# Hybrid attention and MLP block: last ten attention steps reordered, squares added on VectorE, first weights in three groups, unit-matrix products on TensorE before x

## The chip, the cores and the metric

The kernel runs on one core of a Trainium2 chip. The metric is the device time of one execution in microseconds (us), the median of several executions.

## What is computed

One encoder layer for a sequence of 1024 tokens and a model width of 1024, all in float32. The residual stream is normalised, projected to queries, keys and values of two head groups, both groups attend within chunks of 64 tokens, the heads go through one output projection, and a squared-ReLU MLP follows.

```
h = rmsnorm(x, g_pre_mix)
proj = h @ w_in + b_in            # 1024 x 2304: aq, ak, av, bq, bk, bv
out_a = sliding-window attention of 8 heads over 2 chunks, shared keys, a sink per head, bucket bias
out_b = attention of 8 heads over own + 8 previous chunks, bias by clipped relative distance
y = concat(out_a, out_b) @ w_out
x = x + rmsnorm(y, g_post_mix)
h = rmsnorm(x, g_pre_mlp)
y = square(relu(h @ w_up)) @ w_down      # width 4096
out = x + rmsnorm(y, g_post_mlp)
```

## The kernel before

Every engine has its own program, written out by hand as one list of instructions; there is no scheduler. The programs meet at counting semaphores: `wait_ge(s, n)` holds an engine until the semaphore s has reached n. So the order in the code is the order on each engine, and a wait holds all that stands behind it on that engine. A float32 product is made as three products of split operands (`three`, L1621 to L1626): high by high, high by low, low by high. The high part is a rounded copy that ScalarE (ACT) writes, the low part is the difference, which VectorE (DVE) writes.

**First stage.** The sum over the model width goes in eight pieces k of 128 columns. For each k, SyncE (SP) loads 512 KB of x (`load_x`), TensorE (PE) turns its eight 128x128 blocks by products with the unit matrix `ident` into banks 6 and 7 of PSUM (`x_transposes`, T(k) below), ACT writes `x_hi`, DVE writes `x_lo`, and PE makes 18 products of the piece with the first three weight tiles (`first_products`). T(k+1) overwrites the banks that x_hi and x_lo of k are read from, so it waits for x_lo(k). The weights of a piece are 192 KB (`w1_raw`), loaded in two groups by `load_first_weights`: k = 0 and 1 from ACT's queue, k = 2 to 7 from SP's; each is five transfers. ACT also squares x piece by piece (`square`) into two alternating buffers `sq`, which GpSimd (POOL) adds to `sumsq` (L761). A square from k = 3 on waits for the addition two before it. Ahead of the additions POOL's program builds two bias tables, `arow` and `brow`, from small transfers (`relrow`, `t5row`). The sum is reduced (L1140), rooted on ACT and inverted on DVE; its diagonal form `diag` is multiplied on PE (L1662) behind the products of k = 6, after a wait for x_lo of k = 7.

**Attention.** It runs over 64 steps n of one pair of heads and 128 queries: 32 of group A, then 32 of group B, where the keys of a step grow from 128 to 640 over the eight steps of a pair. In each step PE makes the scores of n, `weigh(n-2)` (probabilities by values), and the transposes of the probabilities of n-1, in up to three chunks; between the chunks it makes part of 256 "fills": products of values 2 to 7 and of ten more projection tiles. The fills end with step 53. DVE adds the bias and finds the row's maximum (`scores`), and divides by the row sums (`normalize`); ACT makes the exponentials (`exp`). The transposed chunks are copied out of PSUM by ACT (chunks 0 and 1) and DVE (the last one). Up to step 53 all chunks use bank 6; from step `LATE` = 54 on they rotate over three banks. Scores of group B have one buffer in PSUM: PE's scores(n) wait for DVE's scores(n-1). DVE also takes finished fills out of PSUM (`values`, 320 columns, 12 times; `tile_scaled`, 512 columns, 20 times in the steps), and in the last steps ACT and DVE split the eight pieces of `w_out` (`wo_high`, `wo_low`), at the steps that WO_STEPS lists. Every fourth step ACT stores four finished outputs (`store_mix`).

**After it** come the output projection (`out_steps`, `out_tile`), the norms, and the two MLP products by a scheme of seven products of half-size matrices. The change doesn't touch them.

## Time and profile before

| what | us |
|---|---|
| median of 3 runs | 1135.88 (1135.09 to 1138.67) |
| the profiled execution | 1134.49 |
| its span | 1132.6 |
| TensorE busy | 1078.2 (95%) |
| VectorE busy | 788.1 (70%) |
| ScalarE busy | 473.2 (42%) |
| GpSimd busy | 224.6 (20%) |

The span is what the engines' instructions cover, and 1.9 us lie around it. TensorE does something 95% of the time, so only stretches in which it stands still or in which its granted clock is low have time to give.

### The profile page before, as it was taken

The numbers are of one execution on the slowest core, as the hardware profiler recorded it, in microseconds if no ns is written. First come the engines' busy times: TensorE is split into PE (matmuls) and PEld (weight loads), VectorE is DVE, ScalarE is ACT, GpSimd is POOL, SyncE is SP. The second block draws the span as 40 slices with busy tenths as digits, with TensorE's granted clock in tenths as the row PEclk, the third lists the DMA queues.
The fourth block names the chain that finished last, engine by engine and source line by source line (L and its number), as shares of the span: only waits on it lengthen the run. The fifth ranks groups of instructions, "written<-read, shape, count | busy, mean of one in ns | idle before, by whom it ended". The sixth has DMA issues, their size and how long they took to land.

```text
span 1132.6 us, 16339 instructions
## 1 busy us (share of the span) xinstructions
PE 1078.2 (95%) x5772; PEld 881.2 (78%) x5772; DVE 788.1 (70%) x1634; ACT 473.2 (42%) x951; POOL 224.6 (20%) x195
## 2 busy tenths in 40 slices
PE   6999999999997699998999999999999999999995
PEld 5798877777875588876788888888888888778884
DVE  2754466676766646579898888887544586677797
ACT  4522355544445545584231313131244444344552
POOL 5400000000000000031866667575300000000000
PEclk9999999999998899998999999999999999999998
DMA  9350111111106012221444453535777753354343
GB/s 258 86 173 1 29 30 61 43 38 43 43 1 205 1 60 102 82 92 65 166 141 162 145 168 139 174 133 196 242 251 241 234 148 93 117 181 153 98 117 152
DMA packets 80544, 137.79 MB, mean 122 GB/s; under 512 B 16568, under 2 KB 32960, under 8 KB 78416
## 3 DMA queue, kind: packets, MB, share of 16 engines
q1 hardware_dynamic: 79104, 136.35, 37.3%
q8 instruction: 47, 0.77, 0.3%
q10 hardware_dynamic: 1360, 0.39, 0.2%
q14 instruction: 33, 0.27, 0.1%
HBM read 98.93 MB, written 42.51 MB: 125 GB/s over the span
## 4 chain that ended last, share of the span: by engine, by line
PE 83%; DVE 6%; issue 4%; ACT 3%; POOL 2%; SPq 1%; DMA 1%; ACTq 0%; DVEq 0%; POOLq 0%
PE ps L1624 24%; PE ps L1626 23%; PE ps L1625 23%; PE ps L1747 4%; PE ps L1731 4%; PE ps L1713 3%; ACT prob_b L888 1%; DVE b_lo L1338 1%; PE ps L1825 1%; POOL arow L749 1%; DVE probT_b L1251 1%; SPq L319 1%; DVE wc_lo L1349 1%; DVE tm_lo L1536 1%; DVE sm_lo L1534 0%
## 5 line engine op out<-in xcount | busy, mean ns | idle before, releaser
L1624 PE MATMUL ps<-b_hi,wc_hi 128*128 128x512 f32 x448 | 176.0, 393 | 7.5 <-DVE wc_lo L1349 5.2
L1624 PE MATMUL ps<-tm_hi,sm_hi 128*128 128x512 f32 x448 | 175.1, 391 | 2.8 <-DVE tm_lo L1536 2.5
L1626 PE MATMUL ps<-b_hi,wc_lo 128*128 128x512 f32 x448 | 175.8, 392 | 0.0
L1625 PE MATMUL ps<-b_lo,wc_hi 128*128 128x512 f32 x448 | 175.6, 392 | 0.0
L1626 PE MATMUL ps<-tm_hi,sm_lo 128*128 128x512 f32 x448 | 174.4, 389 | 0.0
L1625 PE MATMUL ps<-tm_lo,sm_hi 128*128 128x512 f32 x448 | 174.4, 389 | 0.0
L1090 ACT ACTIVATE sm_hi<-sm_raw 128x512 fp32r<-128x512 f32 x112 | 70.7, 631 | 152.5 <-DMA sm_raw<-u_matrices 152.5
L1534 DVE TENSOR_TENSOR sm_lo<-sm_raw,sm_hi 128x512 fp32r<-128x512 f32 x112 | 77.1, 689 | 76.4 <-ACT sm_hi L1090 75.9
L1624 PEld LDWEIGHTS ps<-b_hi,wc_hi 128*128 128x128 f32 x448 | 84.9, 190 | 26.8 <-DVE wc_lo L1349 3.8
L1624 PEld LDWEIGHTS ps<-tm_hi,sm_hi 128*128 128x128 f32 x448 | 84.1, 188 | 23.6 <-issue 3.3
L1625 PEld LDWEIGHTS ps<-b_lo,wc_hi 128*128 128x128 f32 x448 | 84.8, 189 | 17.8
L1626 PEld LDWEIGHTS ps<-b_hi,wc_lo 128*128 128x128 f32 x448 | 84.8, 189 | 17.6
L1626 PEld LDWEIGHTS ps<-tm_hi,sm_lo 128*128 128x128 f32 x448 | 84.1, 188 | 17.6
L1625 PEld LDWEIGHTS ps<-tm_lo,sm_hi 128*128 128x128 f32 x448 | 84.1, 188 | 17.2
L1349 DVE TENSOR_TENSOR wc_lo<-wc_raw,wc_hi 128x512 fp32r<-128x512 f32 x64 | 72.1, 1129 | 7.6 <-POOL wc_raw L791 5.5
L1536 DVE TENSOR_TENSOR tm_lo<-w,tm_hi 128x512 fp32r<-128x512 f32 x112 | 76.5, 683 | 0.0
L782 POOL TENSOR_TENSOR wc_raw<-up_raw 128x512 f32<-128x512 f32 x16 | 25.3, 1584 | 251.7 <-PE ps L1794 176.2
L1048 ACT ACTIVATE p1s<-ps 128x512 f32<-128x512 f32 x16 | 9.5, 596 | 154.8 <-PE ps L1626 151.9
L1099 ACT ACTIVATE tm_hi<-w 128x512 fp32r<-128x512 f32 x112 | 69.1, 617 | 0.0
L1624 PE MATMUL ps<-x_hi,wf_hi 128*128 128x512 f32 x160 | 67.6, 422 | 0.1
L1626 PE MATMUL ps<-x_hi,wf_lo 128*128 128x512 f32 x160 | 63.0, 394 | 0.0
L876 ACT ACTIVATE probT_b<-ps 128x512 f32<-128x512 f32 (+3 forms) x48 | 25.9, 540 | 87.6 <-PE ps L1731 87.6
(195 smaller groups left out, 2201.3 us busy)
## 6 DMA issues: line engine op xcount, KB each, us to landing
u_matrices<-stage SPq DMA_DIRECT2D x112, 256.0 KB, 2.4
sm_raw<-u_matrices SPq DMA_DIRECT2D x112, 256.0 KB, 2.6
up_raw<-in_w_up SPq DMA_DIRECT2D x16, 1024.0 KB, 5.9
w<-in_w_down SPq DMA_DIRECT2D x64, 256.0 KB, 3.8
xraw<-in_x SPq DMA_DIRECT2D x8, 512.0 KB, 6.3
w_raw<-in_w_in SPq DMA_DIRECT2D x8, 512.0 KB, 3.5
xr<-in_x SPq DMA_DIRECT2D x8, 512.0 KB, 3.5
x_rows<-xr SPq DMA_DIRECT2D x8, 512.0 KB, 2.6
```

Source lines behind the costliest of these rows:

```text
L876: nc.scalar.activation(dst, src, ACT.Copy).then_inc(s_pta, 1)
L1090: nc.scalar.activation(sm_hi[r][:], sm_raw[r][:], ACT.Copy).then_inc(s_shi, 1)
L1099: nc.scalar.activation(tm_hi[r][:], down_weights[q][c][:], ACT.Copy).then_inc(s_thi, 1)
L1349: nc.vector.tensor_tensor(wc_lo[s][p][:], src, wc_hi[s][p][:].bitcast(F32), ALU.subtract).then_inc(s_wlo[s], 1)
L1534: nc.vector.tensor_tensor(sm_lo[r][:], sm_raw[r][:], sm_hi[r][:].bitcast(F32), ALU.subtract).then_inc(s_slo, 1)
L1536: nc.vector.tensor_tensor(tm_lo[r][:], down_weights[q][c][:], tm_hi[r][:].bitcast(F32), ALU.subtract).then_inc(s_tlo, 1)
L1624: pe.matmul(out, w_hi_, x_hi_, start=start, stop=False)
L1625: pe.matmul(out, w_hi_, x_lo_, start=False, stop=False)
L1626: return pe.matmul(out, w_lo_, x_hi_, start=False, stop=stop)
L1713: last = pe.matmul(score_of(n, hh)[:, c * width:(c + 1) * width], q[rows, tok], k[rows, keys], start=(i == 0), stop=(i == 2))
L1731: last = pe.transpose(ps[:, bank, i * P:(i + 1) * P], prob_of(n, hh)[:, c0 + k * P:c0 + (k + 1) * P], ident[:])
L1747: last = pe.matmul(ps[64 * hh:64 * hh + 64, 7, (t % 4) * P:(t % 4) * P + P], v_tok[:, t + 1 - nk + k, at + 64 * hh:at + 64 * hh + 64], pro ...
```

## The change

It has six parts. (1) PE multiplies the unit matrix by itself 14 times before T(0) and 24 times between T(0) and T(1), into a bank that the first real product overwrites. (2) The first weights are loaded in three groups, k = 0, k = 1 and 2, and k = 3 to 7, and SP's loads stand in another order. (3) ACT and DVE split the weights of k = 0 before they touch x(0). (4) The seven additions of squares move from POOL to DVE. (5) In all attention steps DVE empties finished fills before it works on the scores. (6) From step 54 on PE transposes before it weighs, ACT makes both exponentials before it copies a chunk, and DVE copies its chunk before it normalises; WO_STEPS puts five pieces of w_out, not three, behind the last step.

The tables and the loads of SP:

```diff
-WO_STEPS = (55, 57, 59, 61, 63, 64, 64, 64)
+SQUARES = ((0,), (1,), (2, 3), (4,), (5, 6), (7,), (), ())
+
+WO_STEPS = (59, 61, 63, 64, 64, 64, 64, 64)
...
-            k0, k1 = ((0, 2), (2, KT))[g]
+            k0, k1 = ((0, 1), (1, 3), (3, KT))[g]
...
             load_first_weights(sp, 1)
+            load_x(2)
+            load_x(3)
+            load_first_weights(sp, 2)
+            for k in range(4, KT):
+                load_x(k)
             sp.dma_start(relrow[:, 0:513], rel).then_inc(s_tab, 16)
             sp.dma_start(t5row[:], t5).then_inc(s_tab, 16)
-            for k in range(2, KT):
-                load_x(k)
```

ACT, first stage (`first_hi`, which is new, stands once ahead of the wait for x and then behind it), and attention:

```diff
+            def first_hi(k):
+                act.wait_ge(s_w1[(k >= 1) + (k >= 3)], 80)
+                nc.scalar.activation(w1_hi[:, k], w1_raw[:, k], ACT.Copy).then_inc(s_w1hi, 1)
...
             for k in range(KT):
+                if k == 0:
+                    first_hi(0)
                 act.wait_ge(s_xt, k + 1)
                 nc.scalar.activation(x_hi[:, k], two(6), ACT.Copy, scale=g1[:, k:k + 1]).then_inc(s_xhi, 1)
-                act.wait_ge(s_w1[k >= 2], 80)
-                nc.scalar.activation(w1_hi[:, k], w1_raw[:, k], ACT.Copy).then_inc(s_w1hi, 1)
...
+                if k:
+                    first_hi(k)
...
-                if 1 <= n <= STEPS:
+                if 1 <= n < LATE:
                     copy_chunk(n - 1, 0)
...
-                    for c in range(1, len(chunks_of(n - 1))):
+                    for c in range(0 if n >= LATE else 1, len(chunks_of(n - 1))):
```

DVE, first stage (the same addition leaves POOL's program; `first_lo` goes as `first_hi`), and attention:

```diff
+            def add_squares(k):
+                dve.wait_ge(s_sq, k + 1)
+                if k >= 2:
+                    dve.wait_ge(s_acc, k - 1)
+                total = sumsq[:].rearrange("p t n -> p (t n)")
+                nc.vector.tensor_tensor(total, total, sq[:, k % 2], ALU.add).then_inc(s_acc, 1)
...
+                if k >= 2:
+                    for n in SQUARES[k - 1]:
+                        add_squares(n)
...
-                if n < STEPS:
-                    scores(n)
...
                 if n < STEPS:
+                    scores(n)
+                if n >= LATE:
+                    copies_of(n - 1)
+                if n < STEPS:
                     for hh in range(2):
                         normalize(n, hh)
```

PE, first stage and attention:

```diff
+            def keep_awake(times):
+
+                for _ in range(times):
+                    pe.transpose(ps[:, 0, 0:P], ident[:], ident[:])
+
             pe.wait_ge(s_id, 2)
+            keep_awake(14)
             x_transposes(0)
+            keep_awake(24)
...
-                if n >= 2:
+                if 2 <= n < LATE:
                     weigh(n - 2)
...
+                if n >= LATE:
+                    weigh(n - 2)
```

Three places show how the order moves. The first is DVE's program for k = 2 to 5 of the first stage; before:

```order
L1133 SCALAR_TENSOR_TENSOR x_lo<-ps,small,x_hi 128x1024
L1136 TENSOR_TENSOR w_lo<-w_raw,w_hi 128x384
L1133 SCALAR_TENSOR_TENSOR x_lo<-ps,small,x_hi 128x1024
L1136 TENSOR_TENSOR w_lo<-w_raw,w_hi 128x384
L1127 TENSOR_TENSOR wv_lo_108<-wv_raw_100,wv_hi_92 128x640
```

and with the change, k = 2 to 4 (wv_lo are the low parts of the value weights):

```order
L1150 SCALAR_TENSOR_TENSOR x_lo<-ps,small,x_hi 128x1024
L1135 TENSOR_TENSOR w_lo<-w_raw,w_hi 128x384
L1143 TENSOR_TENSOR sumsq<-sumsq,sq 128x1024
L1150 SCALAR_TENSOR_TENSOR x_lo<-ps,small,x_hi 128x1024
L1135 TENSOR_TENSOR w_lo<-w_raw,w_hi 128x384
L1143 TENSOR_TENSOR sumsq<-sumsq,sq 128x1024 x2
L1150 SCALAR_TENSOR_TENSOR x_lo<-ps,small,x_hi 128x1024
L1135 TENSOR_TENSOR w_lo<-w_raw,w_hi 128x384
L1143 TENSOR_TENSOR sumsq<-sumsq,sq 128x1024
L1130 TENSOR_TENSOR wv_lo_108<-wv_raw_100,wv_hi_92 128x640
```

One or two additions of 1024 columns now stand behind each w_lo, and one of them stands ahead of the reduction of the sum. The second place is PE's program of steps 62 and 63; before, the second half of the scores (bk, bq), weigh (probT_b by v_tok) and then the transposes (ident, prob_b):

```order
L1713 MATMUL ps<-bk_hi_57,bq_hi_53 128x320 x2
L1713 MATMUL ps<-bk_lo_59,bq_hi_53 128x320 x2
L1713 MATMUL ps<-bk_hi_57,bq_lo_55 128x320 x2
L1747 MATMUL ps<-probT_b,v_tok 64x128 x10
L1731 MATMUL ps<-ident,prob_b 128x128 x10
L1713 MATMUL ps<-bk_hi_57,bq_hi_53 128x320 x2
```

and with the change:

```order
L1745 MATMUL ps<-bk_hi_57,bq_hi_53 128x320 x2
L1745 MATMUL ps<-bk_lo_59,bq_hi_53 128x320 x2
L1745 MATMUL ps<-bk_hi_57,bq_lo_55 128x320 x2
L1763 MATMUL ps<-ident,prob_b 128x128 x10
L1779 MATMUL ps<-probT_b,v_tok 64x128 x10
L1745 MATMUL ps<-bk_hi_57,bq_hi_53 128x320 x2
```

The transposes of step n-1 no longer stand behind weigh(n-2) and its waits. The third place is ACT's program of steps 61 to 63; before:

```order
L876 ACTIVATE probT_b<-ps 128x512
L888 ACTIVATE prob_b,small<-prob_b,small 128x640 x2
L876 ACTIVATE probT_b<-ps 128x512
L900 ACTIVATE wo_hi<-wo_raw 128x1024
L895 ACTIVATE mix<-ps 128x4x128
L876 ACTIVATE probT_b<-ps 128x512
L888 ACTIVATE prob_b,small<-prob_b,small 128x640 x2
L876 ACTIVATE probT_b<-ps 128x512 x2
L888 ACTIVATE prob_b,small<-prob_b,small 128x640 x2
```

and with the change:

```order
L891 ACTIVATE prob_b,small<-prob_b,small 128x640 x2
L879 ACTIVATE probT_b<-ps 128x512 x2
L903 ACTIVATE wo_hi<-wo_raw 128x1024
L898 ACTIVATE mix<-ps 128x4x128
L891 ACTIVATE prob_b,small<-prob_b,small 128x640 x2
L879 ACTIVATE probT_b<-ps 128x512 x2
L891 ACTIVATE prob_b,small<-prob_b,small 128x640 x2
```

The two exponentials of a step (L888, then L891) stood between the copies of the chunks 0 and 1 (L876), and now stand ahead of both.

## Rows read from the trace of the kernel before

**Rows 1.** Windows: busy us and count of each engine, granted clock, DMA share, GB/s

```profile
0.00:11.50 11.50, 3.44 (x15) 3.10 (x16) 1.90 (x3) 4.07 (x5) 0.86 (x7) 1.00 0.97 217
...
51.60:341.20 289.60, 285.00 (x2063) 230.05 (x2061) 178.71 (x660) 129.75 (x332) 4.19 (x20) 1.00 0.15 49
341.20:398.90 57.70, 39.62 (x367) 31.65 (x367) 38.10 (x119) 30.17 (x67) 0.00 (x0) 0.86 0.33 101
398.90:500.00 101.10, 101.10 (x488) 84.04 (x487) 60.56 (x141) 59.72 (x118) 7.24 (x5) 1.00 0.26 93
...
363.00:375.00 12.00, 9.51 (x58) 7.08 (x59) 9.13 (x30) 4.87 (x13) 0.00 (x0) 0.61 0.01 1
```

**Rows 2.** Waits of TensorE, 341.2 to 398.9 us: total, times, longest

```profile
PE ps L1747 <- DVE probT_b L1251: 10.7, 8, 2.9
PE ps L1747 <- ACT mix L895: 4.6, 2, 2.6
PE ps L1731 <- ACT probT_b L876: 2.1, 2, 1.4
```

**Rows 3.** Waits of TensorE, 51.6 to 341.2 us

```profile
PE ps L1624 <- DVE v_tok L1185: 1.7, 4, 0.6
```

**Rows 4.** Timeline of the first stage: start, length, engine, instruction, idle time before it

```profile
5.29 1.94 PE L1633 MATMUL ps<-ident,xraw 128*128 128x128 f32 x8 [5.29 <-DMA xraw<-in_x]
...
9.77 0.52 ACT L841 ACTIVATE w_hi<-w_raw 128x384 fp32r<-128x384 f32 x1 [1.33 <-DMA w_raw<-in_w_in]
...
10.00 1.94 PE L1633 MATMUL ps<-ident,xraw 128*128 128x128 f32 x8 [2.77 <-DVE x_lo L1133]
...
14.32 0.55 DVE L1136 TENSOR_TENSOR w_lo<-w_raw,w_hi 128x384 fp32r<-128x384 f32 x1
...
20.34 2.56 DVE L1136 TENSOR_TENSOR w_lo<-w_raw,w_hi 128x384 fp32r<-128x384 f32 x1
...
25.36 1.06 ACT L828 ACTIVATE sq<-xraw 128x1024 f32<-128x1024 f32 x1 [4.90 <-POOL sumsq L761]
...
41.63 1.03 PE L1633 MATMUL ps<-ident,xraw 128*128 128x128 f32 x8
...
45.52 1.21 DVE L1140 TENSOR_REDUCE small<-sumsq 128x8 f32<-128x1024 f32 x1
...
46.60 1.04 PE L1633 MATMUL ps<-ident,xraw 128*128 128x128 f32 x8
...
49.80 1.27 DVE L1133 SCALAR_TENSOR_TENSOR x_lo<-ps,small,x_hi 128x1024 fp32r<-128x1024 f32 x1
...
51.61 1.88 PE L1662 MATMUL ps<-diag,ones 128*128 128x512 f32 x4
```

**Rows 5.** Groups by line of GpSimd, 0 to 60 us

```profile
L761 POOL TENSOR_TENSOR sumsq<-sumsq,sq 128x1024 f32<-128x1024 f32 x7 | 17.6, 2509 | 2.4 <-ACT sq L828 1.7
...
L752 POOL TENSOR_SCALAR brow<-relrow 8x384 f32<-8x384 f32 x1 | 1.2, 1163 | 0.0
```

**Rows 6.** Timeline of the late steps, one engine at a time

```profile
342.52 0.82 DVE L1228 CUSTOM_DVE_ANT_0 prob_b<-ps,bias_b 128x640 f32<-128x640 f32 x1
...
378.36 0.82 DVE L1228 CUSTOM_DVE_ANT_0 prob_b<-ps,bias_b 128x640 f32<-128x640 f32 x1
...
380.79 0.82 ACT L888 ACTIVATE prob_b<-prob_b,small 128x640 f32<-128x640 f32 x1
...
383.22 0.42 DVE L1251 COPY probT_b<-ps 128x256 f32<-128x256 f32 x1
383.98 1.23 DVE L1255 TENSOR_TENSOR wo_lo<-wo_raw,wo_hi 128x1024 fp32r<-128x1024 f32 x1 [0.34 <-ACT wo_hi L900]
...
384.58 1.31 PE L1747 MATMUL ps<-probT_b,v_tok 128*64 128x128 f32 x20 [2.59 <-ACT mix L895]
385.82 1.31 PE L1731 MATMUL ps<-ident,prob_b 128*128 128x128 f32 x10
...
398.94 0.78 PE L1624 MATMUL ps<-wo_hi,mixr_hi 128*128 128x512 f32 x1
```

More of the change, by code:

```diff
@@ L406, in build @@
         s_xlo = sem("x_lo_ready")
-        s_w1 = [sem(f"first_weights_landed{n}") for n in range(2)]
+        s_w1 = [sem(f"first_weights_landed{n}") for n in range(3)]
         s_w1hi = sem("first_weights_hi_ready")
@@ L755, in _ @@
                                     ).then_inc(s_rows, 1)
-            for k in range(1, KT):
-                pool.wait_ge(s_sq, k + 1)
-                if k >= 2:
-                    pool.wait_ge(s_acc, k - 1)
-                nc.gpsimd.tensor_tensor(sumsq[:].rearrange("p t n -> p (t n)"), sumsq[:].rearrange("p t n -> p (t n)"),
-                                        sq[:, k % 2], ALU.add).then_inc(s_acc, 1)
             for p in range(8):
@@ L833, in value_hi @@
                 nc.scalar.activation(wv_hi[k][:], wv_raw[k][:], ACT.Copy).then_inc(s_wvhi, 1)
-            squares = ((0,), (1,), (2, 3), (4,), (5, 6), (7,), (), ())
+            def first_hi(k):
+                act.wait_ge(s_w1[(k >= 1) + (k >= 3)], 80)
+                nc.scalar.activation(w1_hi[:, k], w1_raw[:, k], ACT.Copy).then_inc(s_w1hi, 1)
             act.wait_ge(s_g1, 16)
             for k in range(KT):
+                if k == 0:
+                    first_hi(0)
                 act.wait_ge(s_xt, k + 1)
                 nc.scalar.activation(x_hi[:, k], two(6), ACT.Copy, scale=g1[:, k:k + 1]).then_inc(s_xhi, 1)
-                act.wait_ge(s_w1[k >= 2], 80)
-                nc.scalar.activation(w1_hi[:, k], w1_raw[:, k], ACT.Copy).then_inc(s_w1hi, 1)
-                for n in squares[k]:
+                if k:
+                    first_hi(k)
+                for n in SQUARES[k]:
                     square(n)
@@ L1128, in value_lo, with first_lo @@
                                         ).then_inc(s_wvlo, 1)
+            def first_lo(k):
+                dve.wait_ge(s_w1hi, k + 1)
+                nc.vector.tensor_tensor(w1_lo[:, k], w1_raw[:, k], w1_hi[:, k].bitcast(F32), ALU.subtract
+                                        ).then_inc(s_w1lo, 1)
+            def add_squares(k):
[4 more added lines that the diff above has]
+                nc.vector.tensor_tensor(total, total, sq[:, k % 2], ALU.add).then_inc(s_acc, 1)
             dve.wait_ge(s_g1, 16)
             for k in range(KT):
+                if k == 0:
+                    first_lo(0)
                 dve.wait_ge(s_xhi, k + 1)
@@ L1134, in _ @@
                                                in1=x_hi[:, k].bitcast(F32), op0=ALU.mult, op1=ALU.subtract).then_inc(s_xlo, 1)
-                dve.wait_ge(s_w1hi, k + 1)
-                nc.vector.tensor_tensor(w1_lo[:, k], w1_raw[:, k], w1_hi[:, k].bitcast(F32), ALU.subtract
-                                        ).then_inc(s_w1lo, 1)
+                if k:
+                    first_lo(k)
+                if k >= 2:
+                    for n in SQUARES[k - 1]:
+                        add_squares(n)
                 if k == KT - 2:
@@ L1251, in copy_chunk, with copies_of @@
                 nc.vector.tensor_copy(dst, src).then_inc(s_ptd, 1)
+            def copies_of(n):
+                for c in range(len(chunks_of(n))):
+                    if not chunks_of(n)[c][2]:
+                        copy_chunk(n, c)
             def wo_low(k):
@@ L1277, in _ @@
                         tile_lo(m - V_HALVES + 2 * FIRST_TILES)
-                for c in range(len(chunks_of(n - 1)) if n else 0):
-                    if not chunks_of(n - 1)[c][2]:
-                        copy_chunk(n - 1, c)
+                if 1 <= n < LATE:
+                    copies_of(n - 1)
                 for j in range(FILL_TILES):
```

## The prediction

> **What bounds the kernel now.** First I read the windows [rows 1], which give busy time and granted clock of TensorE (PE) by stage. From 51.6 to 341.2 us it is busy 285.0 of 289.6 us, and behind 398.9 us it is full: 101.1 of 101.1. What these stretches hold can only move as a block. The late attention steps, 341.2 to 398.9 us, are different: 39.62 busy of 57.70, so 18.1 us stand still, at a mean granted clock of 0.86; between 363 and 375 us it is 0.61. Then I read the waits of that stretch [rows 2]: 15.3 of its us are `weigh` waiting, 10.7 for the copy of a chunk by VectorE (DVE) and 4.6 for `store_mix` on ScalarE (ACT). The reader is to see that the engine named is not slow; PE's program has put weigh(n-2) ahead of the transposes of n-1, and DVE's copy stands behind its normalisation. In the middle PE waits 1.7 us for fills to leave PSUM [rows 3]. Last comes the timeline of the first stage [rows 4]: PE starts T(0) when x(0) lands (5.29), T(1) at 10.00 behind x_lo(0), and from there every piece costs 46.60 - 41.63 = 4.97 us if nothing stops PE. Something does: ACT stood 4.90 us before the square at 25.36, held by POOL's additions, with x_hi of the next piece queued behind it.
>
> **First stage.** The end of the stage is the product with `diag` at 51.61 [rows 4].
>
> Loads. ACT's five transfers for k = 0 and 1 landed at 9.77. At a mean 217 GB/s over the first 11.5 us [rows 1] that is about 2.1 MB, in which two pieces of x (1.0 MB), 0.4 MB of ACT's group and 0.6 MB of SP's are seen to be under way. With groups of one and two pieces some 1.4 MB stand ahead of k = 0's last byte, so I estimate its landing at 7.0 us (6 to 8.5: it shares the queues with x(1)). This matters, because ACT now waits for it ahead of x_hi(0). T(0) ends at 5.29 + 1.94 = 7.23 in any case, so the new wait costs about 0.3 us (nothing to 1.7): w_hi 0.5, x_hi 1.1, x_lo 1.3 give x_lo(0) at about 10.1, where T(1) starts today.
>
> Unit-matrix products. T(0) has 8 in 1.94 us, or 0.24 each; 14 of them are 3.4 us and hide before 5.29. The 24 behind T(0) cost 5.8 us at that pace and would hold T(1) until 13.0; at the pace of T(7), 8 in 1.04, they cost 3.1 and end at 10.3. The truth lies between, since the ends overlap: I take T(1) at 10.1 and keep 11.7 for the range. Behind it the clock is up: T(1) costs 1.0, not 1.94, and the 18 long products of k = 0 take 4.1 us, as any piece's do (4.97 less some 0.85 for the next T). T(2) then starts near 15.0, and at 4.97 a piece T(7) at 39.8 instead of 46.60: 6.8 us to win if PE is never held.
>
> Additions. On POOL one takes 2.51 us [rows 5]. On DVE the nearest row is wo_lo, same size and both inputs in SBUF: 1.23 us [rows 6]. DVE's list for a piece is x_lo 1.3, w_lo 0.5, one or two additions, and from k = 4 a wv_lo of 0.8: 5.0 us at most in a period of 4.97. It just fits. But ACT's second square of a piece waits for an addition (squares 3, 6, 7), and x_hi of the next piece stands behind it on ACT. Walking the lists: x_hi is 0.4 us late at k = 3, 1.0 at k = 5, 1.7 at k = 6. PE has about 1.5 us of slack, so T(7) slips by 0.1 only. What is late next is the tail: the reduction stood 45.52 - 41.63 = 3.9 us behind T(6) and now has the later x_lo(6) and an addition ahead of it (2.9 us more), and x_lo(7), which PE needs before `diag`, is behind the reduction, root and diag in DVE's list. It ended at 51.07 with PE at 51.61, so 0.5 us of slack; of 6.8 us won 4.5 stay. PE waits some 2.3 us there.
>
> The port. w_lo of 384 columns took 2.56 us at 20.34, while POOL ran `brow`, and 0.55 at 14.32 [rows 4]. By the Trainium skill, "SBUF — State Buffer", section "Who interferes with whom", a DVE instruction with two SBUF inputs contends with a GpSimd instruction that reads SBUF, and the one that starts second blocks; the additions are of that kind. By it the additions that meet the tables would stretch; without it they cost 1.23. The rows bound it: two `brow` instructions of 1.16 us [rows 5] delay DVE by at most 2.3 us once, now near 31 us where PE's slack takes most. I take 0.5 us. First stage: 4.5 - 0.5 = **4.0 us won**, between 1.5 and 6.8.
>
> **Middle steps.** DVE's program before fill n was: wait for PE's scores, then empty the fill. Now it empties first, while it waits. The fills are done on PE before the scores, so this fits the wait. At most the 1.7 us of [rows 3] come back. At worst each of 12 value halves (about 0.45) and 20 tile halves (0.69) delays a chain: 19 us; but PE was busy 98.4% of this stretch, and the probabilities of a step were ready some 2.6 us before PE reached their transposes. I take **0.8 us won**.
>
> **Late steps.** The cycle today, by [rows 6]: DVE's scores(61) start at 378.36, and the first exponential could start 0.9 us later, but ACT has the copy of chunk 0 of step 60 ahead of it, for which PE's transposes must run: 380.79, 1.6 us late. Then PE holds at weigh(60) until 384.58, and the transposes of 61, whose probabilities were ready at 383.2, start at 385.82.
>
> New cycle of a full step, from DVE's scores start s: second half done s + 1.6; exponentials 0.85 to 2.6; DVE copies its chunk until 1.95, normalises until 2.7 and 3.45. PE: scores of the next step from 1.65 to 2.85 (weigh and transposes take 1.24 each, from 384.58 to 385.82 and on), transposes from 3.1 (ACT's copies free the bank) to 4.4, weigh to 5.7, and again scores. Period 5.7 - 1.65 = about 4.1 us, set by PE. In a step with wo_low (59, 61, 63) ACT's wo_hi ends at s + 4.6 and DVE goes on at 5.8: period 5.8. Steps 56 to 59 have few keys and take 2.6 to 4.8.
>
> Step 54 pays first. The chunks of step 53 still share bank 6, and their copies are now behind ACT's exponentials: transposes at 342.3, 345.7 and 346.9, and DVE normalises only at 347.7 (345.6 today). Its PE idles 2.8 us. From there, with scores(54) at 342.5, the DVE scores of 55 to 63 start at 350.0, 353.3, 356.6, 359.1, 361.7, 366.5, 369.9, 375.7 and 379.0. The last transposes follow at 382.4, weigh(62) at 383.8, and the output projection when wo_low(2) and the low half of mix are made, 386.1, instead of 398.94: 12.8 us. Five pieces of w_out behind the last step cost nothing: DVE makes one in 1.2 us, PE uses one in six products of 512, about 1.4 us, and has weigh(63) to do as well.
>
> Against it stands the clock. Gaps of 2 to 2.6 us in today's late steps were followed by a granted clock of 0.61 over twelve us [rows 1]. The walk has gaps of 2.8 us (step 54) and 1.9 us (step 60), and at 1.2 GHz the 3.7 us of PE work in a step become 7.4. The Trainium skill, "TensorE: Matmul & The Clock Gate", Part 1, says that the clock is throttled by default and activity releases it; so a stage with fewer gaps should keep it, and here the rows agree that it falls behind gaps. I take 2 us off (0 to 5). Late steps: **10.8 us won**, between 6 and 15; 18.1, all idle time, is the ceiling.
>
> **Sum**, on the profiled execution's own time: 1134.49 - 4.0 - 0.8 - 10.8 = 1118.9, so 1119. The median of the runs lies 1.4 us above that execution, which is inside the runs' own spread. Behind 398.9 nothing changes and PE is full, so the block moves up whole.
>
> **Rivals.** (a) As walked, both ends gain: 1119, 1113 to 1125. Chance 0.60. (b) Everything overlaps better, clock up throughout and no wait for `diag`: 1134.5 - 6.8 - 1.7 - 15 = 1111. For it: PE's work in the late steps is under 39.6 us. Against: DVE's list with wo_low. 0.14. (c) The late clock stays at half, or the copies hold the transposes in most steps: late gain 5, so 1134.5 - 4 - 0.8 - 5 = 1125. 0.12. (d) DVE's additions and POOL's tables get in each other's way: each addition that meets the 9 us of tables stretches as w_lo did, by 2.0 us; some four do, three of them feed ACT's squares, and the first stage gains nothing: 1134.5 - 11.6 = 1123. For it: w_lo at 20.34. Against: the short `arow` instructions, running since 13.8, did not stretch w_lo at 14.32. 0.07. This is the case in which the rule of the SBUF page decides. (e) It does nothing: a transfer or table with a fixed time catches the shifted block, 1134. Against: SP's later loads wait for semaphores of the engines that move with it. 0.04. (f) Slower: step 54's pattern repeats in all ten late steps, because both exponentials stand ahead of the copies that free a bank. Price 2.1 us a step, with today's waits kept: 1134.5 - 4.8 + 21 = 1151. It decides when a bank comes free later than the probabilities are ready; with three banks I get 0.3 us, not 2. 0.03.
>
> **Numbers.** What a measurement of this kernel can tell from no change is about 0.3%, 3.4 us. Faster by more than that are (a) to (d) and nothing of (e): 0.93; within, 0.04; slower, 0.03. The range reaches from (b) to (c) and a little past: 1111 to 1127.
>
> **What would show it.** T(1) near 10 us and T(7) near 40, both with products at 0.23 us pitch; PE idle about 2 us before the product with `diag`; DVE additions at 1.2 us; no ACT wait on additions over 2 us. In the late steps: weigh no longer waits, exponentials start 0.9 us behind DVE's scores, the stage from PE's scores(54) to the first output product lasts 45 us, not 57.7, and step 54 is the longest wait. I am wrong if T(1) starts after 12 us, if the late stage is longer than 52 us, or if the span from the first output product to the end changes by over 1 us.

## The result: 20 us faster, 1.7%

| | before | after |
|---|---|---|
| median | 1136.39 (4 runs, 1135.09 to 1138.67) | 1116.23 (4 runs, 1115.60 to 1119.44) |
| ratio | | 0.9826, 95% interval 0.9801 to 0.9851 |
| the profiled execution | 1134.49 | 1116.27 |
| its span | 1132.6 | 1114.4 |

The forecast was 1119.0 in a range of 1111 to 1127. Timed a second time (e10 below) the changed kernel took 1120.05 us, 14.9 less than the kernel before beside it, so the change is worth 15 to 20 us. The two profiled executions differ by 18.2 us. First the engines' busy time in the changed kernel, with its share of the span:

```profile
PE 1075.4 (97%) x5810; PEld 879.5 (79%) x5810; DVE 795.6 (71%) x1641; ACT 475.1 (43%) x951; POOL 209.8 (19%) x188
```

TensorE's busy time is nearly that of before, unit products and all; its share rises because the span shrank around it. To see where, I read four places in each trace: the first value product (the first after the first stage), PE's scores of step 54, the first output product, and the end.

| us | before | after | gain |
|---|---|---|---|
| first value product | 57.45 | 54.94 | 2.5 |
| from there to PE's scores(54) at 341.19 and 336.21 | 283.74 | 281.27 | 2.4 |
| from there to the first output product (the late stage) | 57.75 | 45.71 | 12.0 |
| from there to the end of the span (the rest) | 733.66 | 732.48 | 1.2 |

Windows of the changed kernel (busy us and count of PE, PEld, DVE, ACT and POOL, granted clock, DMA share, GB/s), which answer to [rows 1]. The first has the length of the middle window there, but starts inside the first stage; the second is the late stage exactly:

```profile
46.00:336.00 290.00, 284.83 (x2064) 230.56 (x2063) 183.07 (x671) 131.61 (x335) 4.21 (x20) 1.00 0.16 51
...
336.21:381.92 45.71, 36.88 (x367) 28.63 (x367) 35.01 (x118) 29.29 (x66) 0.00 (x0) 0.93 0.42 128
```

The late stage runs the same 367 products as in [rows 1]. PE now stands still for 8.8 of its us, not 18.1, and its work takes 36.9 us instead of 39.6 because the granted clock is 0.93 instead of 0.86. So 9.3 us of the 12.0 are waits that went, and 2.7 us are the same products at a higher clock.

**Late steps.** PE's waits of the changed kernel, 336 to 392 us:

```profile
PE ps L1763 <- ACT probT_b L879: 4.8, 5, 2.7
PE ps L1745 <- DVE small L1247: 2.4, 3, 1.8
PE ps L1649 <- issue: 1.3, 1, 1.3
PE ps L1763 <- DVE prob_b L1262: 0.2, 1, 0.2
```

Against [rows 2] the 15.3 us of `weigh` are gone: no row of L1779 is left here (in e1, e2, e5 and e10 `weigh` has one wait of 0.6 us). What waits now are transposes, for ACT to free their bank (L1763), and scores, for DVE to empty theirs (L1745), 7.2 us together. The timelines show the two longest. The columns are start, length, engine and instruction, and in brackets the idle time ahead of it and who ended it:

```profile
337.28 0.66 PE L1763 MATMUL ps<-ident,prob_b 128*128 128x128 f32 x4
340.67 0.66 PE L1763 MATMUL ps<-ident,prob_b 128*128 128x128 f32 x4 [2.73 <-ACT probT_b L879]
342.01 0.69 PE L1763 MATMUL ps<-ident,prob_b 128*128 128x128 f32 x2 [0.69 <-ACT probT_b L879]
342.63 2.40 PE L1779 MATMUL ps<-probT_b,v_tok 128*64 128x128 f32 x20
...
364.14 0.41 PE L1745 MATMUL ps<-bk_hi,bq_hi 64*128 64x320 f32 x2 [1.84 <-DVE small L1247]
365.50 2.17 PE L1763 MATMUL ps<-ident,prob_b 128*128 128x128 f32 x10 [0.21 <-DVE prob_b L1262]
```

The first is step 54, whose transposes of step 53 share one bank. The weighing behind it takes 2.40 us, where the same 20 products take 1.31 in [rows 6]: half clock (1.2 of 2.4 GHz) after the gap. The second gap belongs to a step with `wo_low`, and the transposes behind it run slowly too (2.17 against 1.31). In DVE's and ACT's timelines of the same steps the new order is seen:

```profile
337.53 0.82 DVE L1247 CUSTOM_DVE_ANT_0 prob_b<-ps,bias_b 128x640 f32<-128x640 f32 x1
...
343.26 0.55 DVE L1262 TENSOR_SCALAR prob_b<-prob_b,small 128x640 f32<-128x640 f32 x1
...
361.36 1.23 DVE L1279 TENSOR_TENSOR wo_lo<-wo_raw,wo_hi 128x1024 fp32r<-128x1024 f32 x1 [0.63 <-ACT wo_hi L903]
362.51 0.82 DVE L1247 CUSTOM_DVE_ANT_0 prob_b<-ps,bias_b 128x640 f32<-128x640 f32 x1
...
365.93 0.82 DVE L1247 CUSTOM_DVE_ANT_0 prob_b<-ps,bias_b 128x640 f32<-128x640 f32 x1
```

```profile
366.80 0.83 ACT L891 ACTIVATE prob_b<-prob_b,small 128x640 f32<-128x640 f32 x1 [1.21 <-DVE small L1247]
```

DVE's scores(61) start at 365.93 and the exponential 0.87 us behind, where [rows 6] had 378.36 and 380.79, 2.4 us apart. `wo_low` at 361.36 holds the scores at 362.51, and those hold PE until 364.14.

**First stage.** PE's timeline of the changed kernel:

```profile
1.53 3.25 PE L1680 MATMUL ps<-ident 128*128 128x128 f32 x14 [1.53 <-POOL ident L748]
4.95 1.97 PE L1658 MATMUL ps<-ident,xraw 128*128 128x128 f32 x8 [0.17 <-DMA xraw<-in_x]
6.71 3.17 PE L1680 MATMUL ps<-ident 128*128 128x128 f32 x24
11.33 1.07 PE L1658 MATMUL ps<-ident,xraw 128*128 128x128 f32 x8 [1.45 <-DVE x_lo L1150]
...
16.37 1.03 PE L1658 MATMUL ps<-ident,xraw 128*128 128x128 f32 x8
...
48.99 1.98 PE L1694 MATMUL ps<-diag,ones 128*128 128x512 f32 x4 [1.92 <-DVE x_lo L1150]
...
54.94 0.30 PE L1649 MATMUL ps<-wv_hi,x_hi 128*128 128x320 f32 x1
```

The 14 unit products lie ahead of T(0), the 24 end at 9.88, and T(1) is not held by them: it waits 1.45 us longer for x_lo(0). T(2) follows after 5.04 us, and T(3) to T(6) every 4.97 to 5.01; T(7) starts at 41.88, against 46.60 in [rows 4]. Then PE waits 1.92 us ahead of `diag`. The chain that ends in T(1) starts here, in ACT's timeline:

```profile
8.34 0.52 ACT L835 ACTIVATE w_hi<-w_raw 128x384 fp32r<-128x384 f32 x1 [3.71 <-DMA w_raw<-in_w_in]
8.77 1.10 ACT L842 ACTIVATE x_hi<-ps,small 128x1024 fp32r<-128x1024 f32 x1
```

The weights of k = 0 landed at 8.3 us.

### The profile page after: what moved, and what is told of

Same layout as the page of the kernel before. It is cut to its first block, busy times and chain, and to the rows that moved or that the text cites. A ratio compares the mean times of both kernels' runs of the same rounds, so it can differ in the third digit from the quotient of the medians.

```text
span 1114.4 us, 16419 instructions
## 1 busy us (share of the span) xinstructions
PE 1075.4 (97%) x5810; PEld 879.5 (79%) x5810; DVE 795.6 (71%) x1641; ACT 475.1 (43%) x951; POOL 209.8 (19%) x188
## 4 chain that ended last, share of the span: by engine, by line
PE 83%; DVE 7%; issue 5%; ACT 3%; POOL 1%; DMA 1%; ACTq 0%; DVEq 0%; POOLq 0%; SPq 0%
PE ps L1649 24%; PE ps L1651 24%; PE ps L1650 23%; PE ps L1779 4%; PE ps L1763 4%; PE ps L1745 3%; DVE b_lo L1363 1%; PE ps L1859 1%; ACT x_hi L842 1%; DVE sumsq L1143 1%; DMA w_raw<-in_w_in 1%; DVE x_lo L1150 0%; DVE wc_lo L1374 0%; DVE xf L1585 0%; DVE tm_lo L1561 0%
## 5 line engine op out<-in xcount | busy, mean ns | idle before, releaser
L987 ACT ACTIVATE wc_hi<-wc_raw 128x512 fp32r<-128x512 f32 x64 | 40.3, 631 | 54.8 <-POOL wc_raw L780 17.7
L1650 PE MATMUL ps<-x_lo,wf_hi 128*128 128x512 f32 x160 | 62.5, 391 | 0.0
```

The costliest lines, as they stand in the source:

```text
L987: nc.scalar.activation(wc_hi[s][p][:], src, ACT.Copy).then_inc(s_whi[s], 1)
L1650: pe.matmul(out, w_hi_, x_lo_, start=False, stop=False)
```

## The experiments

All kernels are read at the same places. "one" is a single execution, otherwise it is the median; where a kernel was timed over several runs its profiled execution gives the other columns. Middle is from the first value product to PE's scores(54).

| kernel | us | diag | first value | middle | late stage | rest |
|---|---|---|---|---|---|---|
| before | 1136.39 | 51.61 | 57.45 | 283.74 | 57.75 | 733.66 |
| after | 1116.23 | 48.99 | 54.94 | 281.27 | 45.71 | 732.48 |
| e1 late order alone | 1123.02 | 49.97 | 55.81 | 283.73 | 46.79 | 735.07 |
| e2 no unit products | 1121.46 one | 50.52 | 56.48 | 281.28 | 46.82 | 735.02 |
| e3 additions alone | 1135.56 one | 49.90 | 55.84 | 283.73 | 60.08 | 734.05 |
| e4 fills first alone | 1132.71 one | 50.08 | 55.93 | 281.33 | 60.98 | 732.56 |
| e5 w_out at the old steps | 1118.33 one | 48.61 | 54.54 | 281.24 | 48.18 | 732.54 |
| e6 loads alone | 1148.32 one | 62.51 | 68.36 | 283.73 | 59.27 | 735.14 |
| e7 step 54 in the old order | 1114.75 one | 48.33 | 55.96 | 281.30 | 43.14 | 732.50 |
| e8 further | 1111.53 | 47.40 | 54.97 | 281.32 | 43.24 | 732.47 |
| e9 high products early | 1109.17 | 46.70 | 51.27 | 281.26 | 42.16 | 732.31 |
| e10 the changed kernel again | 1120.05 | 48.51 | 54.44 | 281.28 | 46.83 | 735.15 |

### e1: the late order alone

The kernel before with part 6 only (DVE's copies ahead of the normalisation too, as in the change):

```diff
-WO_STEPS = (55, 57, 59, 61, 63, 64, 64, 64)
+WO_STEPS = (59, 61, 63, 64, 64, 64, 64, 64)
...
-                if 1 <= n <= STEPS:
+                if 1 <= n < LATE:
                     copy_chunk(n - 1, 0)
...
-                if n >= 2:
+                if 2 <= n < LATE:
                     weigh(n - 2)
...
+                if n >= LATE:
+                    weigh(n - 2)
```

> The kernel before with the late steps in the new order alone (TensorE, ScalarE and VectorE from step 54 on, and the new WO_STEPS). Theory: the three moves of the late steps are worth 12 us by themselves; scores of step 54 start where they did (341.2 us), the first output product starts near 386.7 instead of 398.94, and the time is 1122 to 1124.5. Rival: part of these 12 us needs the other edits (fills emptied first, or a stretch that starts earlier); then the late stage shortens by under 9 us and the time stays over 1126.

Measured: 1123.02 us (1122.28 to 1123.67) beside 1136.05 for the kernel before, ratio 0.9885 (0.9868 to 0.9901). The first output product starts at 386.33, and the late stage takes 46.79 us. The theory holds: the late order by itself brings 11.0 us against the late stage of the kernel before's profile, and 12.7 against the mean of the four kernels of the table that have the old order (59.5). It is the larger part of the change. Two things in the table are not its doing, since its code ahead of step 54 and behind the first output product is that of the kernel before: the first value product is 1.6 us earlier, and the rest is 1.4 us longer. They are taken up below.

### e2: the changed kernel without the unit products

```diff
             pe.wait_ge(s_id, 2)
-            keep_awake(14)
             x_transposes(0)
-            keep_awake(24)
```

> The changed kernel without its 38 products of the unit matrix by itself. Theory: T(1) starts at 11.3 us as before, since it waits for x_lo(0), but the first pieces run at half clock for some 3 us, so that T(2) comes 2 us later and, since nothing behind it has slack against TensorE's own work, the first value product stands 1 to 2.5 us later than 54.94. Rival: the tail of the stage (squares, reduction, root, x_lo(7)) sets its end and hides this; then that product stands within 0.5 us of 54.94.

Measured: the first value product comes at 56.48 instead of 54.94, 1.54 us later. T(1) starts at the same time, 11.31, but PE's timeline shows what follows it:

```profile
5.11 1.94 PE L1658 MATMUL ps<-ident,xraw 128*128 128x128 f32 x8 [5.11 <-DMA xraw<-in_x]
11.31 1.94 PE L1658 MATMUL ps<-ident,xraw 128*128 128x128 f32 x8 [4.26 <-DVE x_lo L1150]
12.90 0.78 PE L1649 MATMUL ps<-x_hi,w_hi 128*128 128x512 f32 x1
13.47 0.63 PE L1650 MATMUL ps<-x_lo,w_hi 128*128 128x512 f32 x1
```

T(1) takes 1.94 us, not 1.07, and the first long products 0.6 to 0.8, not 0.4. T(2) is 1.5 us late (17.90 against 16.37), and that stays to the end of the stage. So the unit products are worth 1.5 us in this pair of executions, and T(1) does not start later for them. The whole kernel took 5.2 us more than the changed one's profiled execution; 1.1 and 2.5 of these arose in the late stage and the rest, where the programs are equal.

### e3: the additions on VectorE alone

The kernel before, with the additions on DVE in the place that the change gives them, the loads and all else as before:

```diff
-            for k in range(1, KT):
-                pool.wait_ge(s_sq, k + 1)
...
+                if k >= 2:
+                    for n in SQUARES[k - 1]:
+                        add_squares(n)
```

> The kernel before with the seven additions on VectorE alone. Theory: ScalarE's wait of 4.9 us for GpSimd's additions shrinks to under 2.5, the later fall of the clock goes, and the first value product moves from 57.45 to about 52.5 to 54.5 us; w_lo no longer takes over 2 us except beside brow. Rival: VectorE's list is now too long (5.0 us in a period of 4.97) and gives it all back; then that product stays at 56.5 us or later.

Measured: 55.84, between what the theory and the rival expected. Against the kernel before's own profile that is a gain of 1.6 us, but e1 and e4, which run the first stage of the kernel before unchanged, have 55.81 and 55.93. The steps inside tell more. T(7) starts at 42.79, against 45.00 in e1, so the squares no longer hold PE as long; and then the product with `diag` waits:

```profile
49.90 1.98 PE L1666 MATMUL ps<-diag,ones 128*128 128x512 f32 x4 [1.93 <-DVE x_lo L1134]
```

It starts at 49.90, in e1 at 49.97. All that is won up to T(7) is given back in the tail, where x_lo(7) stands behind the reduction and the root in DVE's list. The edit brings nothing that shows alone. DVE's w_lo takes 0.55 or 0.56 us in every piece; the collision has moved to POOL's side (see the port, below).

### e4: fills emptied first, alone

```diff
             for n in range(STEPS + 1):
                 done = halves_done(n - 1) if n else []
-                if n < STEPS:
-                    scores(n)
                 for m in done:
...
+                if n < STEPS:
+                    scores(n)
                 if n < STEPS:
                     for hh in range(2):
                         normalize(n, hh)
```

> The kernel before with finished fills emptied ahead of the scores in all steps, and nothing else. Theory: the wait on v_tok cost 2.4 to 2.8 us although the wait rows of TensorE give 1.7, since the weight loads wait too; scores of step 54 start 2.3 to 2.8 us earlier than 341.2 and the first value product stays at 57.45. Rival: what the middle gained beyond 1.7 us came from the first stage; then they start 1.5 to 1.7 us earlier.

Measured: the middle takes 281.33 us instead of 283.74. PE's scores(54) come at 337.26, 3.9 us before those of the kernel before, but 1.5 of it were there at the first value product. The stretch itself is the cleanest measurement of the study: 283.73 or 283.74 in all four kernels without the edit, 281.24 to 281.33 in all eight with it. It is worth 2.4 us.

### e5: the changed kernel with w_out at the old steps

```diff
-WO_STEPS = (59, 61, 63, 64, 64, 64, 64, 64)
+WO_STEPS = (55, 57, 59, 61, 63, 64, 64, 64)
```

> The changed kernel with WO_STEPS as before, so that five pieces of w_out are split inside the late steps and not three. Theory: each piece inside a step costs VectorE 1.2 us and a wait of 0.5 to 1.1 us for ScalarE, so the late stage (scores of step 54 to the first output product, 45.7 us in the changed kernel) lasts 47.5 to 49.5 us. Rival: in the short steps 55 and 57 VectorE has idle time for it; then the stage is within 1 us of 45.7.

Measured: the late stage takes 48.18 us, 2.5 more, as expected. PE's waits from 336 to 384.1 us say where:

```profile
PE ps L1763 <- ACT probT_b L879: 5.0, 6, 2.7
PE ps L1745 <- DVE small L1247: 4.4, 4, 1.8
```

The scores wait 4.4 us for DVE instead of 2.4: two more steps in which `wo_low` stands ahead of the scores. Against the second execution of the changed kernel (e10: 46.83 us, 3.1 of them this wait) the difference is 1.4 us, so the new WO_STEPS are worth 1.4 to 2.5.

### e6: the loads alone

The kernel before, with part 2 only; the additions stay on POOL, behind the two tables:

```diff
-            k0, k1 = ((0, 2), (2, KT))[g]
+            k0, k1 = ((0, 1), (1, 3), (3, KT))[g]
...
             load_first_weights(sp, 1)
-            sp.dma_start(relrow[:, 0:513], rel).then_inc(s_tab, 16)
-            sp.dma_start(t5row[:], t5).then_inc(s_tab, 16)
-            for k in range(2, KT):
-                load_x(k)
+            load_x(2)
+            load_x(3)
+            load_first_weights(sp, 2)
+            for k in range(4, KT):
+                load_x(k)
+            sp.dma_start(relrow[:, 0:513], rel).then_inc(s_tab, 16)
+            sp.dma_start(t5row[:], t5).then_inc(s_tab, 16)
```

> The kernel before with the first weights in three groups and the new order of SP's loads, the additions staying on GpSimd. Theory: the tables' rows now land near 23.5 us, GpSimd builds the tables first, its additions start after 33 us, ScalarE's square of piece 3 waits for them with x_hi(3) behind it, and the stage ends about 10 us later: first value product at 65 us or later, against 57.45. Rival: earlier pieces of x and weights help by themselves; then it stands earlier than 57.

Measured: 1148.32 us, 13.8 more than the profiled execution of the kernel before; the first value product comes 10.9 us later. The waits from 8 to 64 us:

```profile
POOL arow L752 <- DMA t5row<-in_t: 23.1, 1, 23.1
...
ACT sq L831 <- POOL sumsq L764: 15.2, 1, 15.2
...
PE ps L1636 <- DVE x_lo L1136: 15.0, 2, 12.2
```

To be read from the top: POOL's program begins with the tables, whose input now lands behind all of x; the additions stand behind the tables; ACT's square waits 15.2 us for one, with x_hi of the next piece queued behind it; and PE waits 12.2 us for the x_lo that needs it. So the new order of the loads and the move of the additions are one edit: with the tables' input behind x, the additions can't stay behind the tables. An order that leaves the tables' input where it was has not been run.

### e7: the changed kernel, with step 54 in the old order

```diff
-                if 1 <= n < LATE:
+                if 1 <= n <= LATE:
                     copy_chunk(n - 1, 0)
```

and in the same way `n >= LATE` becomes `n > LATE` for DVE's copies, ACT's other chunks and weigh, so that the new order begins when the chunks have three banks.

> The changed kernel with step 54 in the old order on all three engines, the new one from 55 on. Theory: the waits of 2.73 and 0.69 us in step 54 come from the chunks of step 53, which still share one bank, behind two exponentials; with the old order there the late stage shortens from 45.7 to 43 to 44.5 us. Rival: the old order puts its waits (2.1 us for ScalarE's copies) in the same place; then it stays within 0.7 us of 45.7.

Measured: the late stage takes 43.14 us, 2.6 less than in the changed kernel, and its mean clock is 0.96:

```profile
337.26:380.40 43.14, 35.19 (x367) 27.63 (x367) 35.33 (x118) 29.19 (x66) 0.00 (x0) 0.96 0.44 136
```

The theory holds. Of the 2.6 us, 1.7 are the same 367 products at a higher clock (35.19 us against 36.88) and 0.9 are waits. The whole kernel gains only 1.5 us over the changed one, for a reason outside the edit, in PE's timeline:

```profile
48.33 3.57 PE L1694 MATMUL ps<-diag,ones 128*128 128x512 f32 x4 [1.92 <-DVE x_lo L1150]
50.91 1.31 PE L1649 MATMUL ps<-x_hi,w_hi 128*128 128x512 f32 x1
```

PE waited 1.92 us ahead of `diag`, exactly as in the changed kernel, but here the four products behind took 3.57 us instead of 1.98, and the first value product came 7.6 us behind `diag` instead of 5.95. The same wait cost another 1.7 us of clock.

### e8: e7, one more piece of w_out behind the last step, x ahead of the first weights

```diff
-WO_STEPS = (59, 61, 63, 64, 64, 64, 64, 64)
+WO_STEPS = (59, 61, 64, 64, 64, 64, 64, 64)
...
-                if k == 0:
-                    first_hi(0)
                 act.wait_ge(s_xt, k + 1)
...
-                if k:
-                    first_hi(k)
+                first_hi(k)
```

(and so for `first_lo` on DVE).

> The kernel of the run before this one with two more edits: piece 2 of w_out behind the last step, and x_hi(0) ahead of w_hi(0) on ScalarE. Theory: T(1) starts near 10.0 instead of 11.33, and the first value product stands 0.8 to 1.4 us before 54.94; the 1.3 us in front of the first output product go; time 1111 to 1114. Rival: the tail of the first stage and the start of the output projection are set by VectorE's list; then each edit gives under 0.4 us and the time is that of the run before it.

Measured: 1111.53 us (1109.83 to 1113.88), ratio 0.9779 (0.9763 to 0.9796). T(1) moves from 11.33 to 9.77, as expected, and the product with `diag` to 47.40, 1.6 earlier. But again the clock fell behind the wait for it, and at the first value product, 54.97, nothing was left of it, where 0.8 to 1.4 us were expected; the profiled execution is the slowest of the four. The late stage is as long as e7's (43.24 against 43.14), but not because the sixth piece behind the last step did nothing. The wait of 1.3 us ahead of the first output product is gone from PE's rows, as expected, and in this execution PE took 36.60 us for the same 367 products, at a clock of 0.92 instead of 0.96. In e9, which has the same late code and e7's clock (0.96, 35.21 us busy), the stage takes 42.16 us: the edit is worth about 1 us there. The late stage of e8, then of e9:

```profile
336.29:379.53 43.24, 36.60 (x367) 28.71 (x367) 34.22 (x117) 28.07 (x65) 0.00 (x0) 0.92 0.44 135
```

```profile
332.53:374.69 42.16, 35.21 (x367) 27.61 (x367) 34.19 (x117) 28.04 (x65) 0.00 (x0) 0.96 0.46 139
```

### e9: e8, with the products that need no low part ahead of the wait

```diff
                 else:
+                    first_high_products(k)
                     pe.wait_ge(s_xlo, KT)
                     pe.wait_ge(s_diag, 1)
```

`first_high_products` makes the six products of x_hi by w_hi of k = 7, which need neither x_lo(7) nor `diag`; the twelve others follow behind.

> The kernel e8_further with the six high-by-high products of piece 7 moved ahead of TensorE's wait for x_lo(7) and the product with diag. Theory: the wait of 1.9 us there is filled by 1.4 us of work and the clock does not fall behind it, so the first value product follows diag's by 4.5 us instead of 6 to 7.6, and stands at 52 to 53 us instead of 54.97; time 1109 to 1111. Rival: the fall has to do with where the stretch lies and not with the gap; then that product follows at 54 us or later.

Measured: 1109.17 us (1108.38 to 1109.38, five runs) beside 1134.95, ratio 0.9766 (0.9752 to 0.9781). PE's timeline:

```profile
44.83 1.29 PE L1660 MATMUL ps<-x_hi,w_hi 128*128 128x512 f32 x5
46.70 1.98 PE L1703 MATMUL ps<-diag,ones 128*128 128x512 f32 x4 [0.58 <-DVE x_lo L1145]
...
51.27 0.30 PE L1643 MATMUL ps<-wv_hi,x_hi 128*128 128x320 f32 x1
```

The wait is 0.6 us instead of 1.9, and the first value product comes at 51.27, 3.7 us before the changed kernel's and earlier than I expected. Of these, 2.0 are T(1), which starts at 9.32 instead of 11.33, and 1.4 the six products that now stand ahead of `diag`, at 0.23 us each. It is the best version: 26 us under the kernel before, 7 under the changed one's first timing and 11 under its second, which ran beside it. That the filled wait keeps the clock up is not shown by one profile, since five executions kept it behind the full wait too; what speaks for it is that the five times lie within 1.0 us, where e8's four spread over 4.0. The late stage differs from e8's by 1.1 us with the same code, and PE's busy time by 1.4 (35.21 against 36.60).

### e10: the changed kernel again

The same code, run beside e9 to see what repeats.

> The changed kernel once more, to see which of its checkpoints stand still and which move. Theory: T(1) waits for the landing of the first weights and the clock depends on where its gaps fall, so the first value product moves by up to 1.5 us around 54.94 and the rest behind the first output product by up to 2.6 us around 732.5, while the middle stretch (first value product to scores of step 54) stays at 281.3 within 0.1. Rival: the differences in these places come from the edits; then all three repeat within 0.2 us.

Measured: 1120.05 us (1117.78 to 1121.74), ratio 0.9862 (0.9844 to 0.9880), 3.8 us above the first time. First value 54.44 (54.94 the first time), middle 281.28 (281.27), late stage 46.83 (45.71), rest 735.15 (732.48). The rival, all parts within 0.2 us, falls. The 1.1 us of the late stage are not the clock: PE is busy for 36.7 us there, against 36.9, and waits 1.3 us longer, for `store_mix` (0.6) and for DVE's scores (3.1 instead of 2.4). For the rest, here are windows of twenty us, 110 to 130 us behind the first output product, and of ten us, 150 to 160 us behind it, first of the changed kernel's first profile, then of this one:

```profile
491.92:511.92 20.00, 17.25 (x67) 13.15 (x67) 19.30 (x19) 10.24 (x12) 3.30 (x3) 0.91 0.08 23
...
531.92:541.92 10.00, 9.80 (x43) 8.13 (x44) 9.93 (x10) 4.70 (x9) 8.43 (x5) 1.00 0.09 33
```

```profile
492.55:512.55 20.00, 16.37 (x59) 12.66 (x59) 19.27 (x19) 10.24 (x12) 3.34 (x3) 0.83 0.07 15
...
532.55:542.55 10.00, 8.77 (x31) 7.07 (x32) 9.93 (x9) 4.51 (x9) 8.99 (x7) 0.83 0.14 53
```

Here PE is not full: it stands still for 3 us or so between groups of products, and behind that the clock drops in one execution further than in the other, at 59 products against 67 in the same time, and once more at the second place, at 31 against 43. The length of the wait does not decide it: e5 waits 3.6 us at the same place as this execution does, and its rest takes 732.54 us. Over all kernels the rest takes 732.3 to 732.6 us (six of them), 733.7 and 734.1, or 735.0 to 735.2 (four), whatever the edit.

## Why the prediction was right

**Late steps: 10.8 forecast, 12.0 found.** The mechanism is as walked. With the walk shifted by 4.99 us for the earlier scores(54), DVE's scores of 55 to 63 should have started at 345.0, 348.3, 351.6, 354.1, 356.7, 361.5, 364.9, 370.7 and 374.0; they started at 346.47, 349.78, 352.94, 355.27, 357.75, 362.51, 365.93, 371.62 and 374.93. So from step 55 on each period was right within 0.2 us, and the difference was made once: step 55 came 1.5 us late, 1.1 of it by the weighing at half clock (2.40 us for 1.31), and 0.5 of it came back. Step 54 was the longest wait, 2.73 for 2.8; the gap of step 60 was 1.84 for 1.9; the exponential stood 0.87 behind the scores for 0.9. The 2 us that I took off for the clock were 0.8: the walk alone gave a late stage of 44.9 us, it took 45.71. In e1, e2 and e10 the same order took 46.8, close to what the sum with its 2 us says; but in e10 the added 1.1 us are waits and not clock, so that agreement is partly luck. The old order took 57.75 to 60.98 in four kernels and the new one 45.71 to 46.83, so the part is worth 11 to 15 us. That five pieces behind the last step cost nothing holds (e5). What the prediction had seen and not priced was that the first of the ten steps lost what the others won: e7 puts 2.6 us on it. Rival (f) had the mechanism right for that step alone.

**Middle: 0.8 forecast, 2.4 found.** The mechanism is right, and the term was mis-sized: "at most the 1.7 us" was no bound. [Rows 3] are the waits of PE's matmuls, and a product starts with its weight load, which waits by itself. The waits of the weight loads, kernel before, 40 to 342 us, have a row for it that I had not read:

```profile
PEld ps L1624 <- DVE v_tok L1185: 2.9, 5, 0.9
```

Of five waits, 2.9 us; 2.4 came back. In e4 PE's matmuls are left with one such wait of 0.2. Next to nothing was paid for it: PE's waits for the chunks that DVE copies are 1.5 us there, against 1.2 in the kernel before.

**First stage: 4.0 forecast, 2.5 found, and less than that by the edits.** Three steps were off.

The landing of the first weights was put at 7.0 us, from a mean rate by which 1.4 MB are through at 6.5; it was 8.3, within the bounds of 6 to 8.5 (7.8 to 8.3 in the six executions whose ACT waits for it). T(1) started at 11.33, not 10.1. ACT's wait for them is 1.1 of the lost 1.2 us, and e8 shows that it was the step: with x ahead of the weights T(1) starts at 9.77. The unit products did as forecast; the 24 took 3.17 us and held nobody.

T(7) came at 41.88 for 39.8: 1.2 from T(1), 0.2 from periods of up to 5.04 us, and 0.6 from a slip that I had put at 0.1, since ACT's square waited 2.91 us for an addition just before:

```profile
37.73 1.06 ACT L826 ACTIVATE sq<-xraw 128x1024 f32<-128x1024 f32 x1 [2.91 <-DVE sumsq L1143]
```

The tail was right: 1.92 us of wait ahead of `diag` for some 2.3.

The third step is the starting point. I subtracted from 51.61, the product with `diag` in one execution of the kernel before. With the same code it stands at 49.97 in e1 and 50.08 in e4. All of the difference arises between T(4) and T(5): 28.89 to 36.66 behind a wait of 1.49 in that execution, 28.98 to 35.13 behind one of 1.41 in e4. The windows of 28 to 37 us, first of the kernel before, then of e4, have 30 products at a clock of 0.81 against 39 at full clock:

```profile
28.00:37.00 9.00, 7.19 (x30) 5.77 (x31) 6.53 (x5) 5.11 (x6) 8.57 (x4) 0.81 0.24 33
```

```profile
28.00:37.00 9.00, 7.10 (x39) 5.99 (x40) 6.63 (x5) 6.00 (x7) 8.53 (x4) 1.00 0.23 34
```

So 1.6 us of what the prediction put down to PE being held were a fall of the clock that comes in one execution and not in another. Against e1 and e4 (first value products at 55.81 and 55.93) three executions of the changed first stage, 54.94, 54.54 (e5) and 54.44 (e10), gain 0.9 to 1.5 us, and the fourth, 55.96 (e7), gains nothing. By e2 the unit products are all of that gain; moving the additions alone gives nothing (e3), moving the loads alone loses 11 us (e6), and with both moved and no unit products (e2) the first value product stands at 56.48, no earlier than in e1 and e4.

**The port.** DVE's additions took 1.22 us, and two in a row 2.58; one pair, at 36.11 beside `brow`, took 2.85, or 0.3 more than the 2.55 of a pair in e3 with the tables long done. On the other side POOL's 31 `arow` instructions were stretched by the additions that ran beside them, in POOL's timeline of the changed kernel:

```profile
24.47 10.45 POOL L754 TENSOR_SCALAR arow<-t5row 8x165 f32<-8x165 f32 x31 [22.84 <-DMA t5row<-in_t]
34.89 1.16 POOL L757 TENSOR_SCALAR brow<-relrow 8x384 f32<-8x384 f32 x1
```

The same 31 took 6.83 us in the kernel before, and 6.52 in e6, where they run at the same time as here but without additions on DVE:

```profile
24.78 6.52 POOL L752 TENSOR_SCALAR arow<-t5row 8x165 f32<-8x165 f32 x31 [23.15 <-DMA t5row<-in_t]
```

So the two engines did collide, mostly on POOL's side, where nobody waits for the tables. The Trainium skill, "SBUF — State Buffer", section "Who interferes with whom", has the instruction that starts second blocked. Some rows agree: in e3 a `brow` that started at 21.49, 0.03 us behind an addition, took 2.21 us, and the addition its usual 1.22. Others do not: the pair at 36.11 started 0.08 us behind a `brow` of 1.20 us and lost 0.3, and in [rows 4] the w_lo of 20.34, which took 2.56 us, had started 0.3 us ahead of the `brow` beside it (20.61). POOL's starts are rough, so the order within 0.1 us is not certain. Rival (d), which needed 2.0 us for each addition, did not come about.

**The rest: "wrong if it changes by over 1 us".** It changed by 1.2, and that test was badly chosen: the same code gives 732.48 and 735.15 us in two executions (e10). The sentence "PE is full" was read from the first 101 us behind the first output product and does not hold 110 to 160 us behind it.

In sum: 1.5 less at the start, 1.6 more in the middle, 1.2 more in the late steps and 1.2 behind them, which with rounding gives 18.2 found for 15.6 forecast. The mechanisms of the late and middle steps were right; that the sum came out so close is in part luck. 1.6 of the 2.5 us of the first stage and the 1.2 us behind the late steps are the clock of single executions. Without them some 15.4 us are found, in which a first stage 3.1 us short of its term is made up by the 1.6 and 1.2 us that the middle and the late steps had more.

## What to carry to other kernels

When an in-order engine waits, look at what its program puts ahead of the work that is already ready: here it was enough to let transposes go before weighing, exponentials before copies, and emptied buffers before scores; but begin such an order only at the step from which the buffers allow it. A wait of 2 us that can't be avoided should be filled with work that needs less, since it costs its own length and sometimes as much again in clock. Before a few us are credited to an edit, take a stretch whose code is the same in both kernels and see how far it moves by itself.

## What the runs showed of the hardware

- The same wait of 1.9 us ahead of `diag` was followed by four products in 1.98 us in the changed kernel, e2, e3, e5 and e10, and in 3.57 and 2.87 us in e7 and e8. The window of 48 to 56 us has a granted clock of 0.79 in e7 and of 1.00 in the changed kernel. What decides it is open. In the same way the first stage of one and the same kernel differs by 1.6 us (0.81 against 1.00 from 28 to 37 us), and the rest of one and the same kernel by 2.7 us, where the two windows above have 0.83 against 0.91 and 0.83 against 1.00.
- Unit products ahead of the first data kept the clock up and held nothing: T(1) took 1.07 us with them and 1.94 without, after a gap of 1.45 and 4.26 us, and started at 11.33 and 11.31.
- A load of 192 KB that is issued early beside two of 512 KB landed at 7.8 to 8.3 us, although its bytes and those ahead of it would have been through at 6.5 at the mean rate of [rows 1]. Why is not shown.
- Short POOL instructions of 165 columns on 8 partitions were stretched from 6.5 or 6.8 us to 10.45 for 31 of them by DVE additions with two inputs, which in the changed kernel took 1.22 to 1.29 us each beside them.
